# Products into an unread PSUM bank, between TensorE's folds in the opening and around the last norm's sums at the end, in a two-network kernel on one Trainium2 core

## The reference, cut to what matters

```python
def rmsnorm(x, g):
    xf = x.astype(jnp.float32)
    y = xf * lax.rsqrt(jnp.mean(xf * xf, axis=-1, keepdims=True) + RMS_EPS)
    return y.astype(x.dtype) * g
```

## Time and profile before

| | |
|---|---|
| median of three runs | 1929.53 us |
| the profiled execution's own time | 1927.79 us |
| its span | 1925.9 us |
| mean granted TensorE clock | 0.990 |
| PE busy / PEld busy | 1852.0 / 1484.9 us |
| DVE / ACT / POOL busy | 1098.3 / 694.1 / 222.1 us |

### The profile page before, as it was taken

How to read it: one execution, slowest core, us unless ns; L and a number is a source line. 1 busy time by engine, 2 the same in 40 slices (tenths; PEclk the granted TensorE clock), 3 DMA queues, 4 the chain that set the end, 5 groups by cost and what they waited for, 6 DMA issues and landing times. The chain is left out here.

```text
span 1925.9 us, 35700 instructions
## 1 busy us (share of the span) xinstructions
PE 1852.0 (96%) x15294; PEld 1484.9 (77%) x15294; DVE 1098.3 (57%) x1652; ACT 694.1 (36%) x1156; POOL 222.1 (12%) x220
## 2 busy tenths in 40 slices
PE   8999999999999999999999899989989999999997
PEld 6877757688887666778888668878868888888886
DVE  4664354563256787544366887777565645354545
ACT  4334332241223788543222373333222322222342
POOL 4210011140002000120021340000001100000011
PEclk9999999999999999999999999999989999999998
DMA  5334323152223010134431100001042222232221
GB/s 188 108 115 136 127 76 128 44 210 93 74 70 124 20 43 4 45 109 137 135 101 55 47 2 4 3 3 50 24 174 88 99 100 97 90 107 88 77 99 44
DMA packets 42523, 160.73 MB, mean 83 GB/s; under 512 B 4992, under 2 KB 14208, under 8 KB 27776
## 3 DMA queue, kind: packets, MB, share of 16 engines
q1 hardware_dynamic: 28160, 143.78, 21.9%
q10 hardware_dynamic: 14208, 14.68, 2.1%
HBM read 140.36 MB, written 16.78 MB: 82 GB/s over the span
## 5 line engine op out<-in xcount | busy, mean ns | idle before, releaser
L257 DVE TENSOR_TENSOR wlo<-raw,whi 128x2048 fp32r<-128x2048 f32 (+2 forms) x113 | 251.1, 2222 | 178.1 <-ACT whi L248 177.8
L248 ACT ACTIVATE whi<-raw 128x2048 fp32r<-128x2048 f32 (+2 forms) x113 | 209.2, 1851 | 322.3 <-PE ps L283 161.3
L301 PE MATMUL ps<-act_lo,whi 128*128 128x512 f32 x632 | 243.1, 394 | 0.0
L281 PE MATMUL ps<-act_hi,whi 128*128 128x512 f32 x616 | 242.5, 394 | 0.0
L283 PE MATMUL ps<-act_hi,wlo 128*128 128x512 f32 x616 | 240.0, 390 | 0.0
L282 PE MATMUL ps<-act_lo,whi 128*128 128x512 f32 x616 | 239.7, 389 | 0.0
L300 PE MATMUL ps<-act_hi,whi 128*128 128x512 f32 x592 | 235.6, 398 | 0.0
L305 PE MATMUL ps<-act_hi,wlo 128*128 128x512 f32 x632 | 156.7, 390 | 0.0
L301 PEld LDWEIGHTS ps<-act_lo,whi 128*128 128x128 f32 x632 | 120.3, 190 | 25.9 <-issue 1.2
L305 PEld LDWEIGHTS ps<-act_hi,wlo 128*128 128x128 f32 x632 | 119.0, 188 | 24.8
L300 PEld LDWEIGHTS ps<-act_hi,whi 128*128 128x128 f32 x592 | 111.1, 188 | 32.2 <-issue 8.1
(11 more groups left out here) (527 smaller groups left out, 3366.4 us busy)
## 6 DMA issues: line engine op xcount, KB each, us to landing
raw<-stream_in SPq DMA_DIRECT2D x107, 1024.0 KB, 4.9
v_scratch<-v_out ACTq DMA_DIRECT2D x16, 256.0 KB, 3.4
z_scratch<-zt ACTq DMA_DIRECT2D x16, 256.0 KB, 3.0
mlh_v<-v_scratch SPq DMA_DIRECT2D x4, 1024.0 KB, 4.7
mlh_z<-z_scratch SPq DMA_DIRECT2D x16, 256.0 KB, 2.6
cmp_w<-cmp_w_in SPq DMA_DIRECT2D x2, 2048.0 KB, 11.3
z_scratch<-in_zt ACTq DMA_DIRECT2D x16, 256.0 KB, 2.2
mix_g<-z_scratch SPq DMA_DIRECT2D x16, 256.0 KB, 6.9
```

The costliest lines, as they stand in the source:

```text
L248: act.activation(k.whi[b % 2][:, 0:n], k.raw[b % RAW_SLOTS][:, 0:n], ACT.Copy).then_inc(k.hi_done, 1)
L257: dve.tensor_tensor(k.wlo[b % 2][:, 0:n], k.raw[b % RAW_SLOTS][:, 0:n], k.whi[b % 2][:, 0:n].bitcast(F32), ALU.subtract).then_inc(k.lo_don ...
L281: pe.matmul(bank, hi, x_hi, start=(x == 0), stop=False)
L301: pe.matmul(bank, hi, x_lo, start=False, stop=False)
```

## The change

A helper issues products that nobody reads. In the opening one 128 x 128 by 128 x 128 full 32-bit product (identity by ones) goes into bank 2 ahead of each of the eighteen folds, and three with 256 columns follow the last fold; a wait for the constants' load is put ahead of them. At the end two products of 512 columns in the reduced format go into bank 5 ahead of the last sums, one of 256 columns behind the wait for the second half of the squares, and eleven of 512 columns between the last sum and the wait for the diagonal. No operation is removed, and the other engines' code is unchanged.

```diff
--- before.py
+++ after.py
@@ -460,6 +460,12 @@
             self.low(dve, i)
 
 
+def occupy(k, pe, bank, n, weights, columns):
+
+    for _ in range(n):
+        pe.matmul(k.ps[:, bank, 0:columns.shape[-1]], weights, columns, start=True, stop=True, skip_group_check=True)
+
+
 def stage_norm_final(k, norm):
 
     scaled = k.sem("final_scaled")
@@ -475,12 +481,16 @@
 
         @block.tensor
         def _(pe):
+            occupy(k, pe, 5, 2, k.whi[0][:, 0:P], k.act_hi[:, 0, :])
             for h in range(2):
                 pe.wait_ge(norm.last_sq, h + 1)
+                if h:
+                    occupy(k, pe, 5, 1, k.whi[0][:, 0:P], k.act_hi[:, 0, 0:256])
                 for i in (2 * h, 2 * h + 1):
                     last = pe.matmul(k.ps[:, 7, i:i + 1], norm.sq[:, 1, i * P:(i + 1) * P],
                                      k.const("mean_ones")[:, 0:1], start=False, stop=True, skip_group_check=True)
             last.then_inc(norm.last_sum, 1)
+            occupy(k, pe, 5, 11, k.whi[0][:, 0:P], k.act_hi[:, 0, :])
             for h in range(2):
                 pe.wait_ge(norm.diag_done, h + 1)
                 pe.matmul(k.ps[:, 6, h * S // 2:(h + 1) * S // 2], k.const("ones"),
@@ -651,8 +661,10 @@
 
         @block.tensor
         def _(pe):
+            pe.wait_ge(got, 48)
             for u in range(3 * FOLD_OPEN):
                 m, t = u % 3, u // 3
+                occupy(k, pe, 2, 1, k.const("ident"), k.const("ones"))
                 pe.wait_ge(wide_dve if m == 1 else wide_pool, t + 1 if m == 1 else 2 * t + 1 + m // 2)
                 x = 1 if m == 2 else 0
                 pe.matmul(k.ps[:, 5 + x, 8 * t:8 * t + 8], wide[:, u % W, :], wif[:, m, t, :],
@@ -662,6 +674,7 @@
                                      wide[:, (u - 1) % W, :], start=True, stop=True)
                     if t in (3, FOLD_OPEN - 1):
                         last.then_inc(qk_mm, 1)
+            occupy(k, pe, 2, 3, k.const("ident"), k.consts[:, P:3 * P])
 
         @block.vector
         def _(dve):
```

## The result

The changed kernel takes 1937.38 us (median of 7 runs, 1933.44 to 1939.17), beside 1930.08 us for the kernel before in its 7 runs (1927.11 to 1933.38). The ratio is 1.0037, with a 95% interval of 1.0027 to 1.0046: slower by about 7.1 us, 5.2 to 8.9. The profiled execution of after took 1937.38 us too, with a span of 1935.5 us, which is 9.6 more than the one profiled before.

A forecast was written before the change was run, and what follows sets the result against it. TensorE was taken to bound nearly every slice, with ACT's squares and POOL's chain the opening's joint. Opening +5.4 and end +0.3 gave +5.7 us: 1933.5 for the profiled execution, 1935.2 as median, range 1930.0 to 1938.0.

The forecast's parts named there:

- The fold's pitch: Opening folds: each added product costs 0.43 us at the low clock, seventeen unhidden, 7.26 us; last fold ends at 23.60.
- the earlier trace of the mixed stretch: Kernel before, at 623.30 us: TensorE busy 8.10 of 10.10 us at clock 0.50; taken as sign that the folds stay low.
- ACT and POOL behind it: Opening: ACT's first square moves 5.45 us to 23.20, and POOL's last addition ends at 36.13 instead of 31.59.
- the 0.91 us that came back: Opening: POOL's first addition, no longer beside DVE's work, takes 1.30 us instead of 2.21.
- TensorE behind the three wide products: Opening: three products take 2.56 us, tiles 0 and 1 10.9; sums start at 37.05 instead of 31.64, +5.4 us.
- the floor of +4.5: Opening: smallest delay, set by POOL's end at 36.13, if tiles 0 and 1 get the high clock early.
- The end: Last sums to spread: -0.4 us if the clock holds, +1.1 if it falls and returns; +0.3 taken.
- the bad end: End: the eleven products and the spread all run low, +2.8 us in place of +0.3, 1937.7 us; chance 0.08.
- That the rest is carried along: From the opening's sums on, engines follow one another as before, so the opening's shift reaches the end in full.
- The rival of the high clock in the folds: Opening: added products raise the clock near 9.7 us, folds end near 16.9; 1929.1 to 1933.3, middle 1931.5; chance 0.22.
- Its mechanism for a loss: Under the high-clock rival, TensorE pauses from 29.3 to 32.5, the clock falls and tile 2 runs low: +1.7 to +2.7 us.

The follow-up runs named there:

- eighteen narrow: Kernel before plus only the eighteen products between the folds, each moving 8 columns instead of 128: 1933.10 us beside 1929.49, ratio 1.0021.
- eighteen alone: Kernel before plus only the eighteen 128-column products between the folds, without the three wide ones or those at the end: 1934.14 us beside 1929.49, ratio 1.0025.
- opening alone: Changed kernel's whole opening (eighteen between the folds, three wide behind them) with the end of the kernel before: 1934.94 us beside 1929.45, ratio 1.0029.
- end alone: Kernel before plus only the fourteen products at the end, opening unchanged: 1930.26 us beside 1929.49, ratio 1.0006.
- thirty-six: Kernel before plus two 128-column products ahead of each of the eighteen folds: 1938.77 us beside 1929.38, ratio 1.0043.
- three alone: Kernel before plus only the three 256-column products behind the last fold, with the wait: 1930.83 us beside 1929.49, ratio 1.0003.
- two pauses: Kernel before plus four products in the pause before the sparse attention and seven in the next pause: 1928.80 us beside 1929.16, ratio 0.9998.
- five early and eighteen: Kernel before plus the eighteen products between the folds and five 256-column products of zeros from about 2 us on: 1930.87 us beside 1929.38, ratio 1.0011.
- end spread out: Kernel before plus end products spread between and ahead of the last sums, seven instead of eleven behind the last: 1930.14 us beside 1929.38, ratio 1.0001.
- the pause filled: Kernel before plus four 512-column products in TensorE's 4.4 us wait ahead of the sparse attention: 1927.74 us beside 1929.45, ratio 0.9993.

## Why the prediction was right

**The fold's pitch.** Seventeen products unhidden at 0.427 us: forecast 23.60 for the last fold, measured 23.27, and the 0.33 between them is the load that landed 0.32 us earlier. The first was hidden, as said. The width does not matter between 8 and 128 columns (eighteen narrow), and the clock stayed low through the stretch, as the earlier trace rows of the mixed stretch had suggested. Right.

**ACT and POOL behind it.** The square forecast at 23.20 and measured at 22.94; POOL's first addition, now away from DVE's work, expected at 1.3 us and measured at 1.26; its last end forecast at 36.13, measured at 35.81. Right, with the 0.91 us that came back.

**TensorE behind the three wide products.** The sums were to start at 37.05, behind TensorE and not POOL; they start at 37.52. Two errors cancel in part. The three products took 2.3 us and not 2.56 with tile 0 at 25.47 instead of 26.16, and the level, taken to rise as they end, rose two microseconds into tile 0: its eight high products stand from 25.47 to the next line's at 28.45, 2.98 us, where the high level takes 1.81. The first error is worth -0.7 us and the second +1.2. The opening cost +5.8, forecast +5.4. In eighteen alone and opening alone it was +4.6, and +4.9 in eighteen narrow, near the floor of +4.5 that POOL's chain sets. The size of this term depends on when the level rises, and one value for it was too narrow. That +5.4 came so near in this profile is in part luck; by the medians the opening alone is +5.5.

**The end.** The term was +0.3, as the middle of a clock that holds (-0.4) and one that falls (+1.1), with +2.8 as the bad end. The profiles show 9.14 and 10.6 us against 7.9, +1.3 and +2.7, and in no profile did the clock hold. This term was mis-sized: the clock fell in all three profiles that have products at the end, as it had in before, and the three short products ahead of the sums did not alter it. The two cases that the prediction priced at +1.1 and +2.8 are the two that were measured. How large it is over many executions is less clear; the end alone has a median 0.8 us up.

**That the rest is carried along.** The shift of the opening does reach the end, but not to the tenth. The unchanged middle took 1872.3 us against 1869.8, which the forecast did not have. The profiles of the thirteen kernels spread there from 1868.7 to 1875.0, so this is no cost of the change that could be shown from one pair. The 9.6 us between the two profiles owe 2.5 to it; the 7.1 us of the ratio are the better measure.

Forecast 1935.2, measured 1937.38, which is near the top of the range of 1930.0 to 1938.0; +5.7 against +7.1 (5.2 to 8.9).

**The rival of the high clock in the folds**, and with it the sentence of the Trainium skill that activity releases the throttle ("TensorE: Matmul & The Clock Gate"), did not hold for this mixture: TensorE issued without pause from 5.03 to 25.4, and no load of that stretch is shorter than 286 ns, where the high level has 188. It held for the five wide products from 2 us on, and late for thirty-six. The price given to this rival, 1931.5, is close to what five early products made of it, 1930.87, but that kernel has the end of before. Its mechanism for a loss, that an early TensorE pauses and the clock falls in tile 2, was seen with three alone and with two pauses, and not in five early and eighteen or end spread out.

## What to carry to other kernels

An unread product is free only where its engine pauses anyway, or where the stretch that it lengthens still ends before another engine's. Between products bound by their weight loads it costs a full load pair, however few columns it moves, and if others wait for the stretch, as ACT and POOL did here, the whole cost arrives at the end. Before buying a faster clock for a stretch, look at who ends last at its joint: here it was POOL, and TensorE's early finish turned into a pause, behind which the clock fell in some profiles. A pile of filler between a result and the product that needs it must be shorter than the gap at the *low* level, not at the high one.

## What the runs showed that was not expected

Executions of one and the same kernel differ by up to 8 us (1924.67 to 1932.32 in 30 runs of before on one chip), and the thirteen profiles, of kernels whose code between the two ends is the same but for the two with pauses filled, show where. Counted from the first evacuation, all agree within 0.1 us up to 600 us. They part in the opening, as said, and in four stretches where TensorE pauses or its products are small: near 620 to 650, 835 to 890, 1200 to 1430 us, and at the end. The clock is low there for other lengths and at other moments. In the first of them it was low for 10.2 us behind 623.3 in before, for 3.4 in eighteen narrow, and not at all with the pause filled. Behind 1430 us they run in step again for 470 us. So a difference of a few microseconds between two single profiles says nothing in this kernel unless it is read between marks, stretch by stretch.
